# Gathering an expert layer's rows in two halves of slots instead of two halves of row groups, on one Trainium2 core

## The chip, the cores and the metric

The kernel runs on one core of a Trainium2 chip. The metric is the device time of one execution in microseconds (us); of the kernel before, three runs are shown. Engines are called by their names: TensorE (PE in the profile, its weight loads PEld), VectorE (DVE), ScalarE (ACT), GpSimd (POOL) and SyncE (SP, whose queue issues the DMAs).

## The reference

A two-layer encoder trunk over 256 tokens of width 1024. Each layer has a mixer (retention and chunked attention, or sliding-window attention), a hierarchical mixture of experts, and a gated per-layer embedding. The change lies in the mixture of experts:

```python
def hierarchical_moe(h, w_group, b_group, w_router, b_router, w_gate, w_up, w_down):
    t = h.reshape(b * s, d)
    g_logits = t @ w_group + b_group
    g_onehot = one_hot(argmax(g_logits))                    # 1 of 4 groups
    e_logits = einsum('td,dge->tge', t, w_router) + b_router
    top_v, top_i = top_k(einsum('tge,tg->te', e_logits, g_onehot), 2)   # 2 of its 4 experts
    gates = ...                                             # softmax weights, per token and expert
    for gi in range(4):
        hg = einsum('td,edf->tef', t, w_gate[gi])           # 1024 -> 512
        hu = einsum('td,edf->tef', t, w_up[gi])
        act = silu(hg) * hu * gates[:, gi, :, None]
        out = out + einsum('tef,efd->td', act, w_down[gi])  # 512 -> 1024
```

Every token goes to 2 of 16 experts, so there are 512 (token, expert) slots per layer.

## The kernel before, in words

Each engine has a program of its own, written out by hand in the order of its work, and the programs meet at semaphores. The order is fixed on every engine: what stands behind a wait waits too.

**The expert stage.** The router gives every slot a place, sorted by expert. The normalised rows of the tokens (1024 features = 8 row groups of 128, features k, k+8, k+16, ... in group k) are brought into slot order by TensorE: one-hot matrices `PH` (tile `gather_onehots`, tokens x 512 slots, two token tiles `t`) are the moving operand, and the token rows `HSP` (tile `rows_split`, a high and a low part, read in steps of `KD` = 8 elements) the stationary one. A row group takes four matmuls (two token tiles, two parts), of 512 columns each, into a bank of its own. ScalarE and VectorE copy the sums, multiplied by the norm's weights, to `XS` (tile `normalised`). From there ScalarE copies each expert's block of 64 slots to `XE` (tile `expert_rows`), and TensorE runs gate and up (`gate_up`: for each of 8 groups two matmuls, 16 records per half of the groups), turns the hidden rows (`turned`), runs down (`down`) and scatters the outputs back to tokens (`scatter`). All of these but gather and scatter are fp32 matmuls, which the profile shows as two records each.

**The order around the change** (in `experts` of TensorE's program): after the side product (line 926) the gather of groups 0 to 3, token tile 0 (`gathered_first(0)`), the opening of the second tile's sums (`open_sums(1)`, line 935), groups 0 to 3, token tile 1; then the first halves (groups 0 to 3) of gate and up of experts 0 and 1 (`first_rows`), the gather of groups 4 to 7 (`gathered`), the second half of expert 0 (`other_rows(0)`), `spread` (slots and gates broadcast to all partitions), the second half of expert 1. Then the experts follow one another in `step`. Expert 0's block of groups 0 to 3 has copies of its own (`first_block`, 64 columns), since whole evacuations take longer. The one-hots are made by VectorE, 512 wide, token tile 0 and then 1 (lines 1972 and 1973), in front of the low parts of row groups 4 to 7 (`rows_low(1, 4, KD)`, line 1875).

**The weights.** 16 experts x 3 matrices of 2 MiB per layer pass through nine slots of `weights` in SBUF. SP issues their transfers in a fixed order, and each waits until the matrix before it in its slot has been used; experts 0 to 5, 14 and 15 and all down matrices move in pieces of 1 MiB, which wait for half matrices. Two signals count here: `gate_up_halves` (an expert's first four groups are done) and `gate_up_ready` (all eight). For experts 3 and 4 the order is

```python
for half in range(2):
    load_part(3, 1, half)   # reuses expert 0's gate
    load_part(4, 0, half)   # reuses expert 0's up
    load_part(4, 1, half)   # reuses expert 1's gate
    load_part(3, 2, half)   # reuses expert 1's up
```

Ahead of it SP stores the side product (three transfers, `side_first_stored` to `side_third_stored`; it lies where `XS` will be written) and loads expert 2's down matrix outside the slots (`outside` to tile `residual`, the rest to `weights_rest`).

## Time and profile before

| | us |
|---|---|
| median of three runs | 727.9 (726.28 to 727.92) |
| the profiled execution, own time | 727.73 |
| its span, first to last instruction | 725.9 |
| TensorE busy | 706.7 (97%) |
| VectorE busy | 301.5 (42%) |
| ScalarE busy | 166.1 (23%) |
| bytes moved by DMA | 250.87 MB, mean 346 GB/s |

The expert stages take the time from about 147 to 356 us and from about 480 to 689 us of the span. A row of the windows view gives busy time and count for each engine, then the granted TensorE clock (1.00 is 2.4 GHz, 0.50 is 1.2 GHz), the mean busy share of the 16 DMA engines and what they moved. Ends of matmul records are modelled, so starts are the better guide.

### The profile page before, as it was taken

How to read it: one execution, taken by the hardware profiler on the slowest of the kernel's cores; microseconds unless marked ns; L12 is line 12 of the kernel's file. 1: busy time of each engine (PE TensorE's matmuls, PEld its weight loads, DVE VectorE, ACT ScalarE, POOL GpSimd, SP SyncE). 2: the span in 40 equal slices, each digit the busy share in tenths (PEclk: the TensorE clock that was granted, in tenths of full speed). 3: DMA queues.
4: the chain of work that ended last, by engine and by line, in shares of the span. 5: the costliest groups of instructions: out<-in, count | busy, mean ns of one | idle time of the engine just before them, and what ended most of it. 6: DMA issues, size and time to landing. Idle time of an engine off the chain costs nothing.

```text
span 725.9 us, 8170 instructions
## 1 busy us (share of the span) xinstructions
PE 706.7 (97%) x3062; PEld 328.4 (45%) x3062; DVE 301.5 (42%) x717; ACT 166.1 (23%) x395; POOL 26.4 (4%) x47
## 2 busy tenths in 40 slices
PE   9999999999999999989999999999999999989996
PEld 5488454564333333333445545455333333333344
DVE  1213361545437343433322557263535534324324
ACT  3000241432111111110331144252111111112132
POOL 0500000000000000000000000000000000000000
PEclk9999999999999999999999999999999999999999
DMA  9998448889999999999999851489999999999941
GB/s 344 376 285 293 184 174 328 331 310 367 421 409 424 424 431 424 426 418 422 398 381 409 328 197 79 180 284 355 412 412 426 429 422 424 428 420 422 406 164 59
DMA packets 46056, 250.87 MB, mean 346 GB/s; under 512 B 4200, under 2 KB 5448, under 8 KB 25536
## 3 DMA queue, kind: packets, MB, share of 16 engines
q1 hardware_dynamic: 43648, 245.04, 84.4%
q0 software_dynamic: 2048, 5.07, 2.2%
q8 instruction: 26, 0.43, 0.2%
q10 hardware_dynamic: 320, 0.22, 0.1%
q14 instruction: 14, 0.11, 0.0%
HBM read 247.15 MB, written 4.73 MB: 347 GB/s over the span
## 4 chain that ended last, share of the span: by engine, by line
PE 81%; DMA 9%; SPq 5%; issue 2%; DVE 2%; ACT 1%; POOLq 0%; POOL 0%; ACTq 0%; DVEq 0%
PE bank L1024 25%; PE bank L699 24%; PE bank L1041 12%; SPq L454 4%; DMA weights<-in_moe_w_up_dram 4%; PE bank L732 4%; DMA weights<-in_moe_w_down_dram 4%; PE bank L1049 3%; PE bank L983 2%; PE bank L926 2%; PE bank L684 1%; PE bank L1033 1%; DMA weights<-in_even_w_in_dram 1%; PE bank L712 1%; PE bank L770 0%
## 5 line engine op out<-in xcount | busy, mean ns | idle before, releaser
L1024 PE MATMUL bank<-weights,expert_rows 128*64 128x512 f32 x992 | 222.5, 600 | 6.2 <-DMA weights<-in_moe_w_up_dram 6.2
L699 PE MATMUL bank<-weights,normalised 128*128 128x512 f32 (+1 forms) x448 | 191.4, 580 | 0.9 <-DVE normalised L1699 0.7
L1024 PEld LDWEIGHTS bank<-weights,expert_rows 128*64 128x64 f32 x992 | 73.7, 138 | 147.1 <-issue 145.8
L699 PEld LDWEIGHTS bank<-weights,normalised 128*128 128x128 f32 x448 | 83.1, 190 | 91.4 <-issue 88.5
L1041 PE MATMUL bank<-weights,hidden_turned_odd 128*64 128x512 f32 x256 | 58.8, 598 | 0.4 <-DMA weights<-in_moe_w_down_dram 0.4
L1041 PE MATMUL bank<-weights,hidden_turned 128*64 128x512 f32 x224 | 51.5, 598 | 1.3 <-DVE hidden_turned L2029 0.6
L1534 ACT ACTIVATE gate_tanh<-bank 128x256 f32<-128x256 f32 x32 | 12.3, 384 | 175.2 <-PE bank L1024 175.2
L1385 ACT ACTIVATE expert_outputs<-bank 64x512 fp32r<-64x512 f32 (+1 forms) x32 | 18.9, 591 | 117.7 <-PE bank L1041 112.3
L2029 DVE COPY hidden_turned<-bank 128x256 f32<-128x256 f32 x16 | 6.8, 424 | 75.0 <-PE bank L1033 75.0
L2060 DVE TENSOR_TENSOR expert_outputs<-bank,expert_outputs 64x512 fp32r<-64x512 f32 x30 | 20.5, 684 | 41.7 <-ACT expert_outputs L1385 41.5
L2029 DVE COPY hidden_turned_odd<-bank 128x256 f32<-128x256 f32 x16 | 6.8, 424 | 63.3 <-PE bank L1033 63.1
L1041 PEld LDWEIGHTS bank<-weights,hidden_turned_odd 128*64 128x64 f32 x256 | 16.9, 136 | 34.8 <-issue 31.7
L2041 DVE SCALAR_TENSOR_TENSOR spread_gates<-token_slots,router_temps,token_gates 128x512 f32<-128x512 f32 x32 | 24.0, 751 | 12.9 <-ACT token_gates L1526 11.9
L1041 PEld LDWEIGHTS bank<-weights,hidden_turned 128*64 128x64 f32 x224 | 15.2, 136 | 29.2 <-issue 28.9
L732 PE MATMUL bank<-normalised,weights 128*128 128x256 f32 x128 | 28.4, 380 | 0.0
L1049 PE MATMUL bank<-expert_outputs,scatter_onehots 128*128 128x512 f32 x60 | 26.1, 436 | 0.2
L732 PEld LDWEIGHTS bank<-normalised,weights 128*128 128x128 f32 x128 | 24.1, 190 | 3.7 <-issue 0.5
L1049 PE MATMUL bank<-gather_onehots,scatter_onehots 128*128 128x512 f32 x60 | 23.6, 394 | 0.0
L2044 DVE TENSOR_REDUCE slot_gates<-spread_gates 128x1 f32<-128x512 f32 x32 | 21.9, 686 | 1.1
L1385 ACT ACTIVATE expert_rows<-normalised 128x512 f32 (+1 forms) x32 | 19.5, 611 | 10.9 <-issue 6.9
L1033 PEld LDWEIGHTS bank<-constants,hidden 128*128 128x128 f32 x64 | 10.1, 206 | 26.3 <-issue 24.7
L1381 ACT ACTIVATE normalised<-bank,norm_weights 128x128 f32<-128x128 f32 x48 | 13.7, 368 | 33.3 <-PE bank L684 33.0
(276 smaller groups left out, 647.1 us busy)
## 6 DMA issues: line engine op xcount, KB each, us to landing
weights<-in_moe_w_down_dram SPq DMA_DIRECT2D x60, 1024.0 KB, 19.6
weights<-in_moe_w_gate_dram SPq DMA_DIRECT2D x32, 1024.0 KB, 8.7
weights<-in_moe_w_up_dram SPq DMA_DIRECT2D x32, 1024.0 KB, 10.1
weights<-in_moe_w_gate_dram SPq DMA_DIRECT2D x16, 2048.0 KB, 16.5
weights<-in_moe_w_up_dram SPq DMA_DIRECT2D x16, 2048.0 KB, 21.0
weights<-in_even_w_in_dram SPq DMA_DIRECT2D x5, 2048.0 KB, 20.4
weights<-in_ple_w_gate_dram SPq DMA_DIRECT2D x4, 2048.0 KB, 31.5
weights<-in_even_w_out_dram SPq DMA_DIRECT2D x2, 2048.0 KB, 32.5
```

The costliest lines, as they stand in the source:

```text
L454: sp.dma_start(dst, src).then_inc(done, 16)
L699: mm = pe.matmul(B[bank][:, 0:width], XT[:, k, tok(t)], w[:, k, :], start=(k == 0), stop=(k == KD - 1))
L732: mm = pe.matmul(B[2 * (u % 2) + pair][:, c * SEQ:(c + 1) * SEQ], w[:, k, tok(2 * pair + c)], XT[:, k, :], start=(k == 0), stop=(k == KD - 1))
L926: mm = pe.matmul(B[4 + 2 * t + half][:, :], PINT[:, k, tok(t)], WPL[k][:, half * 512:(half + 1) * 512], start=(k == 0), stop=(k == 1))
L1024: mm = pe.matmul(bank[j * BLK:(j + 1) * BLK, :].rearrange("p (m f) -> p m f", m=2), rows[:, k, :], W[:, slots, a:a + FF // 2], start=(k == ...
L1033: mm = pe.transpose(B[TURNED_BANK][:, c * P:(c + 1) * P], US[:, c:2 * P:2], ident)
L1041: mm = pe.matmul(bank[half * BLK:(half + 1) * BLK, :], hid[:, 2 * (f % 2) + f // 2, :], rows(f)[:, half * 512:(half + 1) * 512], start=(f ...
L1049: return pe.matmul(B[sum_bank(t, half)][:, :], PT2[:, par, tok(t)], YSPLIT[half][:, par, :], start=False, stop=stop)
L1385: return act.activation(dst, src, ACT.Copy)
L2041: stepped(dve.scalar_tensor_tensor(out=SPREAD, in0=SROW.rearrange("p c s -> p (c s)"), scalar=col, in1=WROW.rearrange("p c s -> p (c s)"), ...
L2044: stepped(dve.tensor_reduce(GATES[:, par:par + 1], SPREAD, AX.X, ALU.add), gates)
L2060: return dve.tensor_tensor(YSPLIT[half][low, par, :], bank[high, :], YSPLIT[half][high, par, :].bitcast(F32), ALU.subtract)
```

## The change

The gather is divided the other way: by slots instead of by row groups. First slots 0 to 255 of all eight groups, in pairs of groups that share a bank; then the whole gate and up of expert 0 (its 64 slots are in place in `XS`, and nothing is copied for it); then slots 256 to 511 of all eight groups; then expert 1's first half, the spread, and its second half. Each matmul has 256 columns, and there are twice as many, since each half uses the stationary operands anew. The one-hots are made in the same halves. Evacuations are 256 wide (16 instead of 8, without the four 64-wide copies per layer). SP issues the transfer to `weights_rest` behind the last side store. `rows_bank`, `in_bank`, `by_act` and `evac_count` say which bank, half of a bank, engine and count belong to a group.

```diff
-def rows_bank(k):
-    return (0, 1, 4, 5, 1, 4, 1, 4)[k]
+def rows_bank(half, k):
+    return ((0, 1, 4, 5), (5, 4, 1, 4))[half][k // 2]
+def in_bank(k):
+    return slice(256 * (k % 2), 256 * (k % 2) + 256)
+def by_act(k):
+    return k in (0, 1, 4, 5)
+def evac_count(half, k):
+    return 4 * half + 2 * (k // 4) + k % 2 + 1
...
 # SP
-                        sp.wait_ge(sem("side_ready"), 4 * l + 4)
+                        sp.wait_ge(sem("side_copied"), 4 * l + 4)
+                        side_half_stored(1)
                         sp.dma_start(XD[:, :], srcs[2][l * NE + 2][0:256, :].rearrange("(p c) d -> p (c d)", c=2))\
                             .then_inc(sem("down2_landed"), 16)
-                        sp.wait_ge(sem("side_copied"), 4 * l + 4)
-                        side_half_stored(1)
...
 # TensorE
-                def gathered_part(k, t):
-                    for part in range(2):
-                        mm = pe.matmul(B[rows_bank(k)][:, :], HSP[part][:, t, k:D:KD], PH[:, t, :], start=(t + part == 0),
-                                       stop=(t + part == TT))
+                def gathered(half, k):
+                    for t in range(TT):
+                        for part in range(2):
+                            mm = pe.matmul(B[rows_bank(half, k)][:, in_bank(k)], HSP[part][:, t, k:D:KD],
+                                           PH[:, t, 256 * half:256 * half + 256], start=(t + part == 0), stop=(t + part == TT))
+                    mm.then_inc(sem("rows_ready"), 1)
+                def gathered_first():
+                    pe.wait_ge(sem("onehots_ready"), 4 * l + 2)
+                    pe.wait_ge(sem("hs_low"), 3 * l + 2)
+                    pe.wait_ge(sem("side_copied"), 4 * l + 2)
+                    for k in range(4):
+                        gathered(0, k)
+                    pe.wait_ge(sem("side_copied"), 4 * l + 4)
+                    open_sums(1)
+                    pe.wait_ge(sem("hs_low"), 3 * l + 3)
+                    for k in range(4, KD):
+                        gathered(0, k)
+                def gathered_second():
+                    pe.wait_ge(sem("onehots_ready"), 4 * l + 4)
+                    for k in range(KD):
+                        if k == 0:
+                            pe.wait_ge(sem("rows_by_dve"), 8 * l + evac_count(0, 7))
+                        elif k == 2:
+                            pe.wait_ge(sem("rows_by_act"), 8 * l + evac_count(0, 5))
+                        elif k == 6:
+                            pe.wait_ge(sem("rows_by_dve"), 8 * l + evac_count(1, 3))
+                        gathered(1, k)
...
+                def first_expert():
+                    wait_unit(u0)
+                    wait_unit(u0 + 1)
+                    gate_up(B[gu_bank(0)], XS[:, :, 0:BLK], pair(u0), lambda: wait_second(u0, u0 + 1), sem("gate_up_halves"),
+                            row_ready=row_in_place).then_inc(sem("gate_up_ready"), 1)
...
-                gathered_first(0)
-                pe.wait_ge(sem("side_copied"), 4 * l + 4)
-                open_sums(1)
-                gathered_first(1)
-                first_rows(0)
-                first_rows(1)
-                for k in range(4, KD):
-                    for t in range(TT):
-                        gathered(k, t)
-                other_rows(0)
+                gathered_first()
+                first_expert()
+                gathered_second()
+                second_expert(0)
                 spread()
-                other_rows(1)
+                second_expert(1)
...
 # ScalarE
+                def rows_evac(half, k):
+                    act.wait_ge(sem("rows_ready"), 16 * l + 8 * half + k + 2 - k % 2)
+                    act.activation(XS[:, k, 256 * half:256 * half + 256], B[rows_bank(half, k)][:, in_bank(k)], ACT.Copy,
+                                   scale=NW[:, kn, k:k + 1]).then_inc(sem("rows_by_act"), 1)
+                act.wait_ge(sem("side_first_stored"), 16 * (l + 1))
+                rows_evac(0, 0)
+                rows_evac(0, 1)
+                for half in range(2):
+                    seed(1, half)
+                act.wait_ge(sem("onehots_ready"), 4 * l + 4)
+                rows_evac(0, 4)
+                rows_evac(0, 5)
...
 # VectorE
-                for t in range(TT):
-                    then(dve.tensor_scalar(TMP[:, t, :], IOTA, S2[:, t, :], None, ALU.is_equal))
-                    dve.scalar_tensor_tensor(out=PH[:, t, :], in0=IOTA, scalar=S1[:, t, :], in1=TMP[:, t, :],
-                                             op0=ALU.is_equal, op1=ALU.add).then_inc(sem("onehots_ready"), 1)
+                def gather_onehots(half):
+                    c = slice(256 * half, 256 * half + 256)
+                    for t in range(TT):
+                        then(dve.tensor_scalar(TMP[:, t, c], IOTA[:, c], S2[:, t, :], None, ALU.is_equal))
+                        dve.scalar_tensor_tensor(out=PH[:, t, c], in0=IOTA[:, c], scalar=S1[:, t, :], in1=TMP[:, t, c],
+                                                 op0=ALU.is_equal, op1=ALU.add).then_inc(sem("onehots_ready"), 1)
+                gather_onehots(0)
+                rows_low(1, 4, KD)
+                gather_onehots(1)
...
+                rows_evac(0, 2)
+                dve.wait_ge(sem("side_second_stored"), 16 * (l + 1))
+                rows_evac(0, 3)
+                rows_evac(0, 6)
+                dve.wait_ge(sem("side_third_stored"), 16 * (l + 1))
+                rows_evac(0, 7)
```

The order on TensorE in layer 0, from the last side matmul (`ple_weights_first`, `weights_rest` are its weights) to expert 1's second half. A row is a line, an operation, its tiles (`normalised` there is `XS`), the output's shape and the count of matmuls. Before:

```order
L926 MATMUL bank<-weights_rest,arena 128x512
L983 MATMUL bank<-gather_onehots,rows_split 128x512 x8
L935 MATMUL bank<-zero_column 128x512 x2
L983 MATMUL bank<-gather_onehots,rows_split 128x512 x8
L1024 MATMUL bank<-weights,expert_rows 64x512 x16
L983 MATMUL bank<-gather_onehots,rows_split 128x512 x16
L1024 MATMUL bank<-weights,normalised 64x512 x8
L1010 MATMUL bank<-constants,router_temps 128x128 x4
L1012 MATMUL bank<-constants,router_temps 128x128 x4
L1024 MATMUL bank<-weights,expert_rows 64x512 x8
```

And now:

```order
L940 MATMUL bank<-weights_rest,arena 128x512
L998 MATMUL bank<-gather_onehots,rows_split 128x256 x16
L949 MATMUL bank<-zero_column 128x512 x2
L998 MATMUL bank<-gather_onehots,rows_split 128x256 x16
L1047 MATMUL bank<-weights,normalised 64x512 x16
L998 MATMUL bank<-gather_onehots,rows_split 128x256 x32
L1047 MATMUL bank<-weights,expert_rows 64x512 x8
L1033 MATMUL bank<-constants,router_temps 128x128 x4
L1035 MATMUL bank<-constants,router_temps 128x128 x4
L1047 MATMUL bank<-weights,expert_rows 64x512 x8
```

Expert 1's first half, which was beside expert 0's, now stands behind all of the gather; expert 0's second half stands ahead of the gather's last 32 matmuls.

SP's queue in layer 0 from the first side store to experts 3 and 4's pieces, each row with what it waits for. Before:

```order
L503 DMA side_product_dram<-normalised 128x1024 [waits side_copied]
L478 DMA residual<-in_moe_w_down_dram 128x1024 [waits hs_low,seeded]
L482 DMA side_product_dram<-normalised 128x512 [waits side_copied]
L510 DMA weights_rest<-in_moe_w_down_dram 128x2048 [waits side_ready]
L482 DMA side_product_dram<-normalised 128x512 [waits side_copied]
L478 DMA residual<-in_moe_w_down_dram 128x1024 [waits hs_low,seeded]
```

And now, with the eight pieces behind it, whose order is as before:

```order
L518 DMA side_product_dram<-normalised 128x1024 [waits side_copied]
L493 DMA residual<-in_moe_w_down_dram 128x1024 [waits hs_low,seeded]
L497 DMA side_product_dram<-normalised 128x512 [waits side_copied] x2
L526 DMA weights_rest<-in_moe_w_down_dram 128x2048
L493 DMA residual<-in_moe_w_down_dram 128x1024 [waits hs_low,seeded]
L469 DMA weights<-in_moe_w_up_dram 128x2048 [waits gate_up_halves]
L469 DMA weights<-in_moe_w_gate_dram 128x2048 [waits gate_up_halves]
L469 DMA weights<-in_moe_w_up_dram 128x2048 [waits gate_up_halves]
L469 DMA weights<-in_moe_w_down_dram 128x2048 [waits gate_up_halves]
L469 DMA weights<-in_moe_w_up_dram 128x2048 [waits gate_up_ready]
L469 DMA weights<-in_moe_w_gate_dram 128x2048 [waits gate_up_ready]
```

Only the transfer to `weights_rest` has moved here; the first two pieces wait for expert 0's first half, the next two for expert 1's, the last two shown for expert 0's second.

## Rows read from the trace of the kernel before

**Rows 1.** The page, busy us (share of the span) and instructions of each engine.
```profile
PE 706.7 (97%) x3062; PEld 328.4 (45%) x3062; DVE 301.5 (42%) x717; ACT 166.1 (23%) x395; POOL 26.4 (4%) x47
```

**Rows 2.** Chain of waits, 130 to 180 us: start us, us, what.
```profile
147.31 1.95 PE bank L983 x8
...
149.66 2.27 PE bank L983 x8
151.94 7.02 PE bank L1024 x32
158.96 4.62 PE bank L983 x16
163.57 3.58 PE bank L1024 x16
...
168.25 0.91 PE bank L1012 x8
```

**Rows 3.** Windows: length, busy us (count) per engine, PE clock, DMA share, GB/s.
```profile
155.00:157.00 2.00, 2.00 (x12) 0.65 (x10) 1.15 (x8) 0.00 (x0) 0.00 (x0) 1.00 0.32 61
157.00:167.00 10.00, 10.00 (x42) 5.63 (x38) 1.50 (x2) 1.80 (x3) 0.00 (x0) 1.00 0.98 402
167.00:169.00 2.00, 2.00 (x18) 1.86 (x16) 0.00 (x0) 0.00 (x0) 0.00 (x0) 1.00 0.56 127
169.00:176.00 7.00, 6.20 (x30) 2.29 (x30) 5.46 (x11) 2.90 (x6) 0.00 (x0) 1.00 0.97 366
...
180.00:350.00 170.00, 166.72 (x754) 60.73 (x752) 71.98 (x152) 29.09 (x54) 0.00 (x0) 0.99 1.01 421
```

**Rows 4.** TensorE's waits for weights: timeline of layer 0, a window, layer 1's waits.
```profile
311.34 8.71 PE L1024 MATMUL bank<-weights,expert_rows 128*64 128x512 f32 x32 [2.72 <-DMA weights<-in_moe_w_up_dram]
...
351.34 1.94 PE L1041 MATMUL bank<-weights,hidden_turned_odd 128*64 128x512 f32 x8 [0.42 <-DMA weights<-in_moe_w_down_dram]
...
311.30:314.80 3.50, 3.46 (x10) 1.20 (x12) 0.00 (x0) 0.00 (x0) 0.00 (x0) 0.52 1.03 426
...
PE bank L1024 <- DMA weights<-in_moe_w_up_dram: 3.0, 2, 2.7
```

**Rows 5.** Loads of gather and scatter (ns min/median/max), then timeline from 149.5 us.
```profile
L983 PEld LDWEIGHTS bank<-gather_onehots,rows_split x64: 312/330/348, 146.7 to 496.6; 128*128 128x128 f32 x64
...
L1049 PEld LDWEIGHTS bank<-gather_onehots,scatter_onehots x60: 187/188/192, 184.8 to 686.9; 128*128 128x128 f32 x60
...
149.59 2.35 PE L983 MATMUL bank<-gather_onehots,rows_split 128*128 128x512 f32 x8
...
149.81 1.81 PEld L983 LDWEIGHTS bank<-gather_onehots,rows_split 128*128 128x128 f32 x7
```

**Rows 6.** Timeline of TensorE, two scatter matmuls that follow one another.
```profile
185.03 0.39 PE L1049 MATMUL bank<-gather_onehots,scatter_onehots 128*128 128x512 f32 x1
185.26 0.40 PE L1049 MATMUL bank<-expert_outputs,scatter_onehots 128*128 128x512 f32 x1
```

**Rows 7.** Timeline of VectorE: one-hots, low parts, evacuation, 256-wide one-hots.
```profile
145.37 0.49 DVE L1972 TENSOR_SCALAR normalised<-normalised,router_temps 128x512 f32<-128x512 f32 x1
...
148.12 0.73 DVE L1875 SCALAR_TENSOR_TENSOR rows_split<-residual,norm_stats,rows_split 128x512 fp32r<-128x512 f32 x1
...
161.33 0.75 DVE L1991 TENSOR_SCALAR normalised<-bank,norm_weights 128x512 f32<-128x512 f32 x1 [5.01 <-PE bank L983]
...
172.65 0.35 DVE L2048 TENSOR_SCALAR spread_gates<-token_slots,router_temps 128x256 f32<-128x256 f32 x1
173.04 0.48 DVE L2049 SCALAR_TENSOR_TENSOR scatter_onehots<-token_slots,router_temps,spread_gates 128x256 fp32r<-128x256 f32 x1
```

**Rows 8.** Timeline of SP's queue: first, second and last pair of issues.
```profile
155.56 0.33 SPq L454 DMA_DIRECT2D weights<-in_moe_w_up_dram  x1
...
159.00 0.33 SPq L454 DMA_DIRECT2D weights<-in_moe_w_up_dram  x1
...
172.76 0.33 SPq L454 DMA_DIRECT2D weights<-in_moe_w_up_dram  x1
```

More of the change, by code:

```diff
@@ L1159, in other_rows @@
-                def other_rows(e):
-                    n = u0 + 3 * e
-                    if e == 1:
-                        pe.wait_ge(sem("xe_ready"), NE * l + 2)
-                    gate_up(B[gu_bank(e)], XS[:, :, 0:BLK] if e == 0 else XE[:, e], pair(n), lambda: wait_second(n, n + 1), None, (1,),
-                            first_block if e == 0 else None).then_inc(sem("gate_up_ready"), 1)
-                gathered_first(0)
-                pe.wait_ge(sem("side_copied"), 4 * l + 4)
-                open_sums(1)
@@ new lines, in second_expert @@
+                def second_expert(half):
+                    n = u0 + 3
+                    if half == 0:
+                        pe.wait_ge(sem("xe_first"), l + 1)
+                        pe.wait_ge(sem("rows_by_act"), 8 * l + evac_count(1, 1))
+                        wait_unit(n)
+                        wait_unit(n + 1)
+                        gate_up(B[gu_bank(1)], XE[:, 1], pair(n), None, sem("gate_up_halves"), (0,))
+                    else:
+                        pe.wait_ge(sem("xe_ready"), NE * l + 2)
+                        gate_up(B[gu_bank(1)], XE[:, 1], pair(n), lambda: wait_second(n, n + 1), None, (1,))\
+                            .then_inc(sem("gate_up_ready"), 1)
@@ L1482, in experts @@
                             seed(0, half)
-                for half in range(2):
-                    seed(1, half)
                 def rows(e, off=None, part=slice(0, KD), done="xe_ready", count=1):
@@ new lines, in experts @@
+                act.wait_ge(sem("side_first_stored"), 16 * (l + 1))
[6 more added lines that the diff above has]
+                rows_evac(0, 5)
+                act.wait_ge(sem("g_below_max"), l + 1)
+                act.activation(RT[:, 20:28], RT[:, 20:28], ACT.Exp).then_inc(sem("g_exp"), 1)
+                act.wait_ge(sem("second_below_first"), l + 1)
@@ L1503, in experts @@
+                act.activation(RT[:, 84:86], RT[:, 84:86], ACT.Exp).then_inc(sem("second_exp"), 1)
                 act.wait_ge(sem("table_ready"), 2 * l + 1)
                 offs = act.value_load(TBL[0:1, 1:2], min_val=0, max_val=LAST)
-                if l == 1:
-                    act.wait_ge(sem("gate_up_ready"), NE * l - 1)
-                for half in range(2):
-                    for k in (4 * half, 4 * half + 2):
-                        if half == 0:
-                            first_block(k)
-                        else:
-                            act.wait_ge(sem("rows_ready"), 8 * l + k + 1)
-                        if k == 0:
-                            act.wait_ge(sem("side_first_stored"), 16 * (l + 1))
-                        rows_evac(k)
-                    act.wait_ge(sem("rows_by_act"), 4 * l + 2 * half + 2)
-                    act.wait_ge(sem("rows_by_dve"), 4 * l + 2 * half + 2)
-                    rows(1, offs, slice(4 * half, 4 * half + 4), ("xe_first", "xe_ready")[half], (1, 2)[half])
-                    if half == 0:
-                        act.wait_ge(sem("g_below_max"), l + 1)
-                        act.activation(RT[:, 20:28], RT[:, 20:28], ACT.Exp).then_inc(sem("g_exp"), 1)
-                        act.wait_ge(sem("second_below_first"), l + 1)
-                        act.activation(RT[:, 84:86], RT[:, 84:86], ACT.Exp).then_inc(sem("second_exp"), 1)
@@ L1524, in experts @@
+                for part in range(2):
+                    rows_evac(1, 4 * part)
+                    rows_evac(1, 4 * part + 1)
+                    act.wait_ge(sem("rows_by_act"), 8 * l + evac_count(1, 4 * part + 1))
+                    act.wait_ge(sem("rows_by_dve"), 8 * l + evac_count(1, 4 * part + 3))
+                    rows(1, offs, slice(4 * part, 4 * part + 4), ("xe_first", "xe_ready")[part], (1, 2)[part])
                 act.wait_ge(sem("srow_ready"), l + 1)
@@ L2067, in low_parts @@
                         low_part(bank, e % 2, half).then_inc(sem("ys_low_ready"), 1)
[L2069 to L2073 removed]
+                for k in (2, 3, 6, 7):
+                    rows_evac(1, k)
                 dve.wait_ge(sem("srow_copied"), l + 1)
```

61 lines of the change are left out of this document (8 added, 53 removed).

## The prediction

> **What bounds the kernel now.** I read the page first, then the chain of waits of layer 0's expert stage, the windows of the same stretch, TensorE's idle rows, and last the single lines. The page says that TensorE is busy 97% of the span [rows 1], so time added to TensorE is time unless it was waiting anyway. The chain from 147 to 169 us [rows 2] is TensorE alone: the gather in three pieces (1.95, 2.27 and 4.62 us = 8.84 us for 32 matmuls), the first halves of experts 0 and 1 (7.02 us, so 3.51 each), expert 0's second half (3.58, to 167.15), the spread (to 168.25 + 0.91 = 169.16, so 2.0 us) and then expert 1's second half. Nothing else ends a step there.
>
> The windows show the second bound [rows 3]. Between 180 and 350 us the DMA engines are full (share 1.01) at 421 GB/s, so a piece of 1 MiB (half of a weight matrix) takes 2.49 us, and nothing lost before that stretch can be made up inside it. Between 155 and 176 us they are not full. Held against 421 GB/s, the four windows lack 2 x (1 - 61/421) = 1.7 us, 10 x (1 - 402/421) = 0.45, 2 x (1 - 127/421) = 1.4 and 7 x (1 - 366/421) = 0.9: 4.5 us of transfer time lost. That the transfers decide the end is seen in TensorE's waits [rows 4]: 2.72 us for expert 13's weights at 311 us, and 0.42 us at 351.34 us for the second half of the last down matrix, the last unit of the layer. So the end of layer 0's expert stage is set by DMA, with no slack at the last unit. After the 2.72 us of idling the granted clock is 0.52, the 1.2 GHz level, for 3.5 us, and that matrix takes 8.71 us, where an undisturbed one takes about 7.1. Layer 1 is the same: 3.0 us of such waits for gate and up weights.
>
> **TensorE's part.** The change replaces 32 gather matmuls of 512 columns by 64 of 256. The stationary operand (128 tokens of one row group, read in steps of eight elements) is the same one in both halves, and each half loads it again: 32 loads become 64. What does such a pair cost? In the steady stretch seven loads begin within 1.81 us including the last one's 0.33, so one every (1.81 - 0.33)/6 = 0.247 us [rows 5]. Is that the moving operand or the load? The scatter moves the same 512 columns of the same type, but its stationary operand is contiguous: its load takes 188 ns where the gather's takes 330 [rows 5], and its matmuls follow one another 0.23 us apart [rows 6]. The gather is slower than the scatter by its load, so the load sets its pace, and halving the columns takes nothing from it. I take 0.246 us for each of the 64. The ends: 0.22 us, if a 256-column matmul disturbs the load less (where no gather matmul runs yet, two loads start 149.81 - 149.59 = 0.22 apart, the first with the group of matmuls [rows 5]); below, half of the scatter's 0.23 with some gap, 0.125, if the load were hidden altogether.
>
> The Trainium skill (TensorE: Matmul & The Clock Gate, section LDWEIGHTS) makes a load cost its columns at 1.2 GHz, 107 ns for 128, whatever its stride, and lets it be pulled ahead of running matmuls; by it a pair would be bound by the 256 moving columns, the gather would cost nothing more, and this is the rival "hidden loads" below. The same skill (SBUF — State Buffer, section Door 1: The DMA port swizzle, its note on cachelines) says that each step to a new 16-byte line pays a penalty; a step of eight fp32 elements is 32 bytes, which is the side that the trace takes.
>
> Now the path. The first gather matmul can start at 147.31 as before: the one-hots are now made 256 wide, and rows of that width take 0.35 and 0.48 us and start 0.39 apart [rows 7], so the four of the first half end at 145.37 + 0.39 + 0.40 + 0.39 + 0.48 = 147.0. The low parts of row groups 4 to 7 (0.73 us [rows 7]) come next, ready at 147.8, wanted near 151.7; the second half's one-hots end near 149.5, wanted at 163. They cost nothing; if VectorE were 0.5 us late there, TensorE would lose just that.
> - Gather, slots 0 to 255: 32 x 0.246 = 7.87, plus 0.41 for opening the sums (the step between the first two gather rows [rows 2]), plus 0.2 for a load that has nothing to hide behind: ends at 155.8.
> - Expert 0 whole, 2 x 3.51: first half done at 159.3 (before 155.5), all at 162.8 (before 167.2). An evacuation of 256 columns can't take longer than the 0.75 us of a whole row group [rows 7]; even so groups 6 and 7, the last, are in place by 157.5, and wanted from 161 on.
> - Gather, slots 256 to 511: 7.87 + 0.2, ends at 170.9. Before, the last 16 matmuls took 4.62 instead of 16 x 0.247 = 3.95 because they waited for banks; the new order of banks takes these waits away, and that is in the sum.
> - Expert 1's first half 3.51 (174.4), spread 2.0 (176.4), second half 3.51: 179.9. Before: 169.15 + 3.51 = 172.66.
>
> TensorE is thus 7.25 us later per layer. The removed 64-wide copies of expert 0 and halved evacuations are ACT's and VectorE's; TensorE did not wait for them, so I cost them at nothing, and the router arithmetic behind them (ends near 159 instead of 155) is wanted only by the spread at 174.
>
> **The DMA queue's part.** SP issues in a fixed order: after experts 3 and 4's pieces that reuse expert 0's first halves come two that reuse expert 1's first halves, and only then those that reuse expert 0's second halves. Before, these were issued at 155.56, 159.00, 167.20 and 172.76 us, two pieces each [rows 8, 3], and data flows some 1.5 us after the issue (61 GB/s until 157). Now: the first two at 159.4, flowing from 160.9 to 165.9; the next not before expert 1's first half is done, 174.5, flowing from 176.0. That expert 0's second halves are free at 162.8, 4 us sooner than before, helps nobody, as they stand behind that wait. From 176 on six pieces keep the engines busy 15 us, and the rest follows in time. Lost: 155.2 to 160.9 and 165.9 to 176.0 = 5.7 + 10.1 = 15.8 us, against 4.5 before. The transfers are **11.3 us** late per layer, 4 us more than TensorE, and since the last unit has no slack, the stage ends 11.3 us later. The 4 us show up as longer waits for weights in experts 11 to 15. The weights_rest transfer, issued behind the side store 0.6 us later, and the last piece of residual, issued 2 us later because ScalarE now opens sums behind the gather, only shift idle time before 155; they are wanted only in expert 2's down step, after experts 0 to 3 have passed.
>
> Sum: 2 x 11.3 = 22.6 us on the profiled execution's 727.73 us, 0.2 below the median shown: **750 us**. With 0.22 us per pair each layer saves 64 x 0.026 = 1.7: 747.
>
> **The rivals.**
> - Hidden loads: a pair takes 0.125. For it speaks that loads run beside matmuls; against it the 330 against 188 ns. TensorE would be 8.0 + 0.4 = 8.4 instead of 8.84 us (and 0.2 from gaps: 0.7 earlier at expert 1's end). The queue would still lose: first issue at 155.3, next at 166.5, idle 155.2 to 156.8 and 161.8 to 168.0 = 7.8 against 4.5, so +3.3 per layer: 734.3.
> - TensorE's lateness fills its own waits: if the transfers were not put off, 7.25 us late would swallow the 3.6 us of waits and the 1.6 us of slow clock, +2.1 per layer: 731.8. Against it: the issue order above.
> - Not slower: pairs below 0.13 us (where 64 x p + 0.4 falls under 8.84) and a queue that stays no tighter than before, so that only TensorE's 0.7 us per layer are left: 726.3. It decides only if both hold; the 4.5 us that the queue lacks now would have to be TensorE's doing alone.
> - New stalls: two groups now share a bank and leave it together. If evacuations hold the gather up as before (0.7 us a layer), and one more stretch at 1.2 GHz (1.6 us a layer) falls behind the last long DMA wait, 750 becomes 755.
>
> **How the numbers follow.** The forecast gets 0.76 (own range 746 to 754), new stalls 0.07, hidden loads 0.09, filled waits 0.04, not slower 0.04. The range 734 to 756 takes in the first three. A difference of 0.3% (2.2 us) is about what a measurement of this kernel tells from none. Only the fourth rival lies below: 0.02 faster, 0.02 same, 0.96 slower.
>
> **What would show it.** Gather loads still near 330 ns and 0.245 apart, 16, 16 and 32 of them in 3.9, 3.9 and 7.9 us. Expert 0's gate and up in one stretch beginning near 155.8. SP issuing at about 159.4 and then nothing until 174.5; two holes in the DMA windows, near 156 to 161 and 166 to 176. TensorE 7 us late at expert 1's end and 11 us late at the end of each expert stage, with DMA waits of 8 us or so instead of 3.6. A pace near 0.13 would make it wrong in the first term, a stage that ends 7 us late or less in the second.

## The result and the profile after

The changed kernel takes **748.08 us** (median of 4 runs, 747.75 to 748.68), the kernel before in the same comparison 727.91 us (4 runs, 726.28 to 729.18). The ratio is 1.0279 with a 95% interval of 1.0258 to 1.0301: 2.8% slower, +20.2 us. The profiled execution took 748.10 us with a span of 746.3 us (before: 727.73 and 725.9), so the two traces differ by 20.4 us. A trace is of one execution; the times are medians of several.

The page of the changed kernel: engines, and the group of the gather's loads (busy us, mean ns, then the idle time before them).

```profile
PE 722.4 (97%) x3126; PEld 346.3 (46%) x3126; DVE 303.2 (41%) x729; ACT 167.1 (22%) x399; POOL 26.4 (4%) x47
...
L998 PEld LDWEIGHTS bank<-gather_onehots,rows_split 128*128 128x128 f32 x128 | 31.3, 337 | 3.3 <-issue 2.1
```

TensorE is busy 15.7 us longer than in [rows 1] and its share is 97% as before: by shares alone nothing changed. The loads are 128 where there were 64, at 337 ns each.

The chain of waits of the changed kernel in layer 0, from the first gather matmul to the spread (start us, us, what), and the first piece of layer 1's gather:

```profile
148.05 3.91 PE bank L998 x16
151.96 0.41 PE bank L949 x2
152.37 4.04 PE bank L998 x16
156.41 7.02 PE bank L1047 x32
163.43 7.90 PE bank L998 x32
171.33 3.58 PE bank L1047 x16
...
176.00 0.91 PE bank L1035 x8
...
491.29 3.90 PE bank L998 x16
```

Held against [rows 2], whose pieces are 1.95, 2.27 and 4.62 us, the gather takes 3.91 + 4.04 + 7.90 = 15.85 us where it took 8.84. No wait for banks stands between the pieces. The one-hots are only just in time:

```profile
147.28 0.48 DVE L1984 SCALAR_TENSOR_TENSOR gather_onehots<-normalised,router_temps 128x256 fp32r<-128x256 f32 x1
```

The last one of the first half is done at 147.76, and the timeline has the first gather record at 147.82; experiment 1, whose one-hots are made as before, takes 3.73 us for the same 16 matmuls, so at most 0.2 us is lost here. Expert 1's second half begins at 176.91 (before: 169.16), and its row of the timeline ends at 180.48 (before: 172.72). Counted from each kernel's own first gather matmul that is 32.43 us, before 172.72 - 147.31 = 25.41: **7.0 us** more.

Windows of the changed kernel (length, busy us per engine, clock, DMA share, GB/s):

```profile
156.00:161.00 5.00, 5.00 (x24) 1.85 (x25) 3.76 (x21) 0.41 (x2) 0.00 (x0) 1.00 0.14 49
161.00:166.00 5.00, 5.00 (x23) 3.22 (x20) 0.00 (x0) 0.40 (x2) 0.00 (x0) 1.00 0.99 362
166.00:176.00 10.00, 10.00 (x49) 7.35 (x49) 1.75 (x4) 2.11 (x6) 0.00 (x0) 1.00 0.10 35
176.00:360.00 184.00, 177.95 (x805) 66.30 (x805) 81.09 (x168) 32.95 (x61) 0.00 (x0) 0.99 1.01 422
```

SP's queue in the same stretch of the changed kernel (each row one issue):

```profile
160.04 0.33 SPq L469 DMA_DIRECT2D weights<-in_moe_w_up_dram  x1
...
174.96 0.33 SPq L469 DMA_DIRECT2D weights<-in_moe_w_up_dram  x1
175.33 0.43 SPq L469 DMA_DIRECT2D weights<-in_moe_w_down_dram  x1
175.81 0.43 SPq L469 DMA_DIRECT2D weights<-in_moe_w_up_dram  x1
```

Two pieces go out at 160 us and then nothing until 174.96, where [rows 8] has issues at 155.56, 159.00, 167.20 and 172.76. The windows show the two holes that follow: 49 GB/s for 5 us and 35 GB/s for 10 us, and full engines (422 GB/s) behind them for 184 us. Expert 0's second halves had been free since 163.43; the piece that goes into one of them is the row of 175.81, 12 us later, behind the two that wait for expert 1's first half.

The rest of the stage on TensorE (timeline of the changed kernel, idle time before the row in brackets):

```profile
292.48 7.09 PE L1047 MATMUL bank<-weights,expert_rows 128*64 128x512 f32 x32 [0.40 <-DMA weights<-in_moe_w_up_dram]
...
307.24 8.79 PE L1047 MATMUL bank<-weights,expert_rows 128*64 128x512 f32 x32 [2.72 <-DMA weights<-in_moe_w_up_dram]
...
322.00 7.09 PE L1047 MATMUL bank<-weights,expert_rows 128*64 128x512 f32 x32 [1.03 <-DMA weights<-in_moe_w_up_dram]
...
346.84 3.65 PE L1047 MATMUL bank<-weights,expert_rows 128*64 128x512 f32 x16 [0.99 <-DMA weights<-in_moe_w_up_dram]
...
361.66 1.94 PE L1064 MATMUL bank<-weights,hidden_turned_odd 128*64 128x512 f32 x8 [0.46 <-DMA weights<-in_moe_w_down_dram]
...
366.49 1.16 PE L698 MATMUL bank<-constants,residual 128*128 128x128 f32 x8 [0.39 <-DVE residual L1718]
```

The five waits for weights sum to 5.6 us; before there were three, 3.6 us: 2.72 and 0.42 [rows 4] and one of 0.45 at 296.59. The stage ends at the last row shown, 218.44 us after the first gather matmul, where before it was 356.18 - 147.31 = 208.87: **+9.57 us**. In layer 1 it is 709.65 - 491.29 = 218.36 against 689.28 - 480.96 = 208.32: **+10.04**. The other 0.75 us of the 20.4 is a shift: the first gather matmul starts at 148.05 and not at 147.31, and the last side matmuls ahead of it are late by as much. It comes from the first 15 us of the span, where both kernels run the same program. The same row of TensorE's timeline, before and now:

```profile
14.41 6.17 PE L699 MATMUL bank<-weights,normalised 128*128 128x512 f32 x14
```

```profile
15.16 5.31 PE L713 MATMUL bank<-weights,normalised 128*128 128x512 f32 x12
```

From that row to the last side matmuls both traces take 131.87 us. Between the layers the two kernels are equal, 123.78 and 123.76 us from the end of layer 0's stage to layer 1's last side matmuls.

### The profile page after: what moved, and what is told of

Read it like the earlier page. It is cut to its first block, busy times and chain, and to the rows that moved or that the text cites. A ratio compares the mean times of both kernels' runs of the same rounds, so it can differ in the third digit from the quotient of the medians.

```text
span 746.3 us, 8308 instructions
## 1 busy us (share of the span) xinstructions
PE 722.4 (97%) x3126; PEld 346.3 (46%) x3126; DVE 303.2 (41%) x729; ACT 167.1 (22%) x399; POOL 26.4 (4%) x47
## 4 chain that ended last, share of the span: by engine, by line
PE 70%; DMA 15%; SPq 10%; issue 2%; DVE 2%; ACT 1%; POOLq 0%; POOL 0%; ACTq 0%; DVEq 0%
PE bank L713 24%; PE bank L1047 18%; SPq L469 10%; DMA weights<-in_moe_w_up_dram 8%; PE bank L1064 7%; DMA weights<-in_moe_w_down_dram 7%; PE bank L998 4%; PE bank L746 4%; PE bank L940 2%; PE bank L1072 2%; PE bank L698 2%; PE bank L726 1%; PE bank L1056 1%; PE bank L852 1%; PE bank L784 0%
## 5 line engine op out<-in xcount | busy, mean ns | idle before, releaser
L1047 PE MATMUL bank<-weights,expert_rows 128*64 128x512 f32 x960 | 215.9, 601 | 10.9 <-DMA weights<-in_moe_w_up_dram 10.9
L998 PEld LDWEIGHTS bank<-gather_onehots,rows_split 128*128 128x128 f32 x128 | 31.3, 337 | 3.3 <-issue 2.1
L998 PE MATMUL bank<-gather_onehots,rows_split 128*128 128x256 f32 x128 | 32.5, 409 | 0.0
L1399 ACT ACTIVATE expert_rows<-normalised 128x512 f32 (+1 forms) x32 | 19.6, 611 | 15.3 <-issue 10.9
## 6 DMA issues: line engine op xcount, KB each, us to landing
weights<-in_moe_w_gate_dram SPq DMA_DIRECT2D x16, 2048.0 KB, 19.6
```

Source lines behind the costliest of these rows:

```text
L998: mm = pe.matmul(B[rows_bank(half, k)][:, in_bank(k)], HSP[part][:, t, k:D:KD], PH[:, t, 256 * half:256 * half + 256], start=(t + part == ...
L1047: mm = pe.matmul(bank[j * BLK:(j + 1) * BLK, :].rearrange("p (m f) -> p m f", m=2), rows[:, k, :], W[:, slots, a:a + FF // 2], start=(k == ...
L1399: return act.activation(dst, src, ACT.Copy)
```

## The experiments

The change does three things at once: it doubles the gather's loads, it leaves SP's order of issues as it was while the order of TensorE's work is another, and it moves one-hots, copies and banks. The experiments undo or do one at a time. Two marks are read in each: the first down matmul (TensorE's lateness at the head of the stage) and the transposes behind the stage (its end), both counted from the start of the last pair of side matmuls ahead of the gather, layer 0 / layer 1. The changed kernel is +7.0 / +7.0 us at the first and +9.6 / +10.0 at the second. Ratios are to the kernel before in the same comparison, with their 95% interval.

**1. Only the loads.** The kernel before, with each 512-column gather matmul as two of 256 that load the same operand; order, banks, copies and queue untouched.

```diff
-    mm = pe.matmul(B[rows_bank(k)][:, :], HSP[part][:, t, k:D:KD], PH[:, t, :], start=(t + part == 0),
-                   stop=(t + part == TT))
+    for n in range(2):
+        c = slice(256 * n, 256 * n + 256)
+        mm = pe.matmul(B[rows_bank(k)][:, c], HSP[part][:, t, k:D:KD], PH[:, t, c], start=(t + part + n == 0),
+                       stop=(t + part + n == TT + 1))
```

> The kernel before, its order untouched, but each gather matmul of 512 columns is two of 256 (64 per layer), so each stationary operand is loaded twice. Theory (the strided load of 0.25 us sets the pace): loads start 0.246 apart, the gather takes about 16 us instead of 8.8, TensorE is 7.2 us late at expert 1's end; the queue's order fits this order of work, so its transfers are as late as TensorE and no more, and the time rises by about 2 x 7 = 14 us to 742. Rival (loads are hidden, the change's loss is all order): no load costs more, 728. Rival (TensorE's lateness fills its own DMA waits): 2 x 2 = 4 us, 732.

Measured: 741.57 us, ratio 1.0199 [1.0184, 1.0215]. First down +6.9 / +6.9, stage end +6.6 / +6.6. Its chain of waits:

```profile
147.62 3.73 PE bank L985 x16
...
151.77 4.06 PE bank L985 x16
155.83 7.02 PE bank L1026 x32
162.85 7.93 PE bank L985 x32
```

Its loads in the view by lines (ns min/median/max):

```profile
L985 PEld LDWEIGHTS bank<-gather_onehots,rows_split x128: 312/337/341, 147.0 to 510.4; 128*128 128x128 f32 x128
```

The pieces are nearly those of the changed kernel. Doubling the loads alone costs 13.9 us of the 20.2, 6.6 per layer, with no change in where the work stands, as expected; both rivals (728 and 732) are out. Here the stage's end is late by no more than TensorE's head. SP's queue says why:

```profile
162.89 0.33 SPq L454 DMA_DIRECT2D weights<-in_moe_w_up_dram  x1
...
174.40 0.33 SPq L454 DMA_DIRECT2D weights<-in_moe_w_up_dram  x1
```

The second pair of pieces goes out at 162.89, as soon as expert 1's first half is read (155.83 + 7.02), and not at 174.96.

**2. Only the queue's order undone.** The changed kernel, with SP's loop split so that the pieces reusing expert 0's halves are issued before any that reuse expert 1's.

```diff
 for half in range(2):
     load_part(3, 1, half)
     load_part(4, 0, half)
+for half in range(2):
     load_part(4, 1, half)
     load_part(3, 2, half)
```

> The changed kernel, but SP issues the pieces that reuse expert 0's second halves ahead of those that reuse expert 1's first halves. TensorE's program is as changed. Theory (the queue's fixed order makes the transfers 4 us later than TensorE): the issues for expert 0's second halves come at about 163.5 instead of 175.8, the hole from 166 to 176 shrinks by 5 us, TensorE is still 7.1 us late at expert 1's end, its later waits fall back to those of before, and the time falls by 6 to 8.5 us to 740 to 742. Rival (TensorE's lateness alone makes the loss, the holes don't matter): 748, no change.

Measured: 741.13 us, 1.0187 [1.0171, 1.0202]; first down +7.0 / +7.0, stage end +7.2 / +6.6. SP's queue of this kernel:

```profile
162.27 0.33 SPq L469 DMA_DIRECT2D weights<-in_moe_w_up_dram  x1
...
173.75 0.33 SPq L469 DMA_DIRECT2D weights<-in_moe_w_up_dram  x1
```

The issues stand where experiment 1 has them, TensorE is as late as in the changed kernel, and 7.0 us are gone (748.08 - 741.13). Of these, 2.4 and 3.4 lie in the two stages, and 1.2 ahead of layer 0's gather, which begins at 146.85 here and at 148.05 in the changed kernel. That part is not the edit's: the row of the changed kernel at 15.16 stands at 13.95 in this trace, and all eleven traces, whose program is the same up to there, lie between the two. By the stages the change's 19.6 us divide into 13.2 for the loads (experiment 1, both layers) and 5.9 for two DMA pieces queued behind a wait that had nothing to do with them (this one). About half a microsecond of the stages is left open. The window from 150 to 176 us puts the same into bytes. Before, experiment 1, experiment 2, and the changed kernel, in this order:

```profile
150.00:176.00 26.00, 25.20 (x116) 13.18 (x117) 11.74 (x36) 7.84 (x18) 0.00 (x0) 1.00 0.88 334
```

```profile
150.00:176.00 26.00, 26.00 (x119) 18.05 (x119) 6.27 (x25) 5.42 (x12) 0.00 (x0) 1.00 0.64 239
```

```profile
150.00:176.00 26.00, 26.00 (x120) 17.75 (x121) 6.39 (x27) 5.15 (x13) 0.00 (x0) 1.00 0.64 233
```

```profile
150.00:176.00 26.00, 26.00 (x117) 18.06 (x117) 6.73 (x32) 5.72 (x14) 0.00 (x0) 1.00 0.47 159
```

At 422 GB/s (the changed kernel's full rate) its 159 against 334 is 26 x 175/422 = 10.8 us of transfer time; experiment 1 lacks 5.9 and experiment 2 lacks 6.2.

**3. The stationary operand laid out contiguously.** The changed kernel, with the split rows stored as (row group, 128 columns) instead of every eighth element. The work of spreading them goes to the engines that write them.

```diff
-HSP = [HL[:, part] for part in range(2)]
+HSP = [HL[:, part].rearrange("p t (k m) -> p t k m", k=KD) for part in range(2)]
...
-    mm = pe.matmul(B[rows_bank(half, k)][:, in_bank(k)], HSP[part][:, t, k:D:KD],
+    mm = pe.matmul(B[rows_bank(half, k)][:, in_bank(k)], HSP[part][:, t, k, :],
...
-act.activation(HSP[0][:, t, :], H[:, t, :], ACT.Copy, scale=rstd(kn, t))
+act.activation(HSP[0][:, t], H[:, t, :].rearrange("p (m k) -> p k m", k=KD), ACT.Copy, scale=rstd(kn, t))
```

> The changed kernel, but the tokens' high and low rows are written group by group, so that a stationary operand of the gather is 128 contiguous elements; nothing else is moved. Theory (the stride makes the load slow): loads fall from 337 to about 190 ns, the matmuls start 0.12 to 0.13 apart, the gather takes 8.2 us instead of 16, TensorE reaches expert 1's end 0.7 us before the kernel before; the queue's order still makes the transfers about 3 us late per layer: 733 to 735. Rival (the number of loads or a floor for 256 columns sets the pace, whatever the stride): 748. Rival (the strided reads of ScalarE and VectorE that now write these rows are slow): loads are fast, but the gather starts later than the side matmuls' end.

Measured: 738.03 us, 1.0141 [1.0126, 1.0157]. First down -0.4 / -0.4, stage end +2.4 / +2.7. Loads and ScalarE's copies by lines (ns min/median/max):

```profile
L998 PEld LDWEIGHTS bank<-gather_onehots,rows_split x128: 186/192/192, 148.2 to 504.3; 128*128 128x128 f32 x128
...
L1482 ACT ACTIVATE rows_split<-residual,norm_stats x4: 2147/2166/2173, 129.9 to 480.5; 128x1024 fp32r<-128x1024 f32 x4
```

The chain of waits at layer 0's gather, and TensorE's timeline ahead of layer 1's stage:

```profile
148.47 1.94 PE bank L998 x16
...
159.95 2.13 PE bank L998 x16
...
162.18 0.89 DVE normalised L1999 x2
```

```profile
473.47 0.40 PE L927 MATMUL bank<-constants,router_temps 128*128 128x20 f32 x2 [1.98 <-DVE router_temps L1889]
473.71 3.66 PE L713 MATMUL bank<-weights,normalised 128*128 128x512 f32 x4
```

The window over those four matmuls has a granted clock of 0.54:

```profile
473.70:477.40 3.70, 3.70 (x7) 1.64 (x7) 1.42 (x6) 0.00 (x0) 0.00 (x0) 0.54 0.02 4
```

The load took 192 ns where it took 337, and 16 gather matmuls 1.94 us instead of 3.91, with everything else of the change in place. That is the direct proof that the stride of the load sets the pace; 7.2 and 7.3 us per layer go with it, and the 2.4 and 2.7 that stay go with the queue's order (experiment 4). With the loads fast the banks begin to matter: ahead of its last 8 matmuls the gather waits 1.0 us, to 163.11, for VectorE's copies out of a bank (`normalised`, the row at 162.18), so the first down matmul is only 0.4 us early. The expected 733 to 735 was missed by 3 us or more, and its second rival, that the engines which now write these rows are slow, came true: ScalarE's copies take 2.17 us where they took 1.16, VectorE's of 512 elements 1.2 where it was 0.75, and they stand ahead of TensorE. Layer 1's stage begins 4.3 us later (TensorE waits 1.98 us for router arithmetic that is queued behind a copy, and the next four matmuls then run at half the clock, 3.66 us against 1.98), layer 0's 0.7 us later: from ScalarE's first copy to the last side matmuls it is 17.57 us, in the traces that leave the copies contiguous 16.83. The strided access was not removed but moved to two other engines, which are slow at it too.

**4. Both.** Experiment 3 with experiment 2's loop.

> The changed kernel with contiguous stationary operands and the other queue order together. Theory: both terms are gone; TensorE 0.7 us earlier at expert 1's end than before the change and the transfers no later, so 726.5, 1 to 2 us under the kernel before. If only one of the two causes were real, the time would be that of the better of the two single runs.

Measured: 731.07 us, 1.0042 [1.0028, 1.0056]. First down -0.4 / -0.4, stage end -0.7 / -0.7: with the loads fast and the queue in order, the stage itself is shorter than before in both layers, and nothing of the +9.6 and +10.0 is left to explain. Against experiment 3 the queue's order alone is worth 3.1 and 3.4 us. The expected 726.5 was missed by the same 0.7 and 4.2 us ahead of the two gathers.

**5. Runs of four elements.** The changed kernel with rows in two blocks of four groups, so that ScalarE and VectorE move runs of four and the load's step is 4 elements instead of 8.

```diff
+HSP = [HL[:, part].rearrange("p t (q m r) -> p t q m r", q=2, r=4) for part in range(2)]
...
+    mm = pe.matmul(B[rows_bank(half, k)][:, in_bank(k)], HSP[part][:, t, k // 4, :, k % 4],
```

> The changed kernel with the token rows kept in two blocks of four row groups, so that a stationary operand is read in steps of four elements (16 bytes) and ScalarE and VectorE read and write runs of four. In e3_contiguous ScalarE's and VectorE's steps of eight elements cost 1 us each time, 1 us of delay ahead of layer 0's gather and 4.3 us ahead of layer 1's. Theory (one step per 16-byte line is still free): loads near 190 ns, ScalarE's rows near 1.2 us, VectorE's near 0.75 per 512, gather matmuls 0.13 apart, and with the queue's order as changed the stages 2.1 to 2.4 us longer than in the kernel before (as in e3): 732 to 733. Rival (only steps that hit a line twice are free): loads stay at 330 ns and the time near 748.

Measured: 747.51 us, 1.0277 [1.0262, 1.0293], the changed kernel again. Its loads and copies:

```profile
L998 PEld LDWEIGHTS bank<-gather_onehots,rows_split x128: 308/332/334, 147.0 to 513.2; 128*128 128x128 f32 x128
...
L1482 ACT ACTIVATE rows_split<-residual,norm_stats x4: 1149/1162/1162, 129.4 to 483.4; 128x1024 fp32r<-128x1024 f32 x4
```

The expected 732 to 733 was missed, and the rival (748) held: the load is as slow with a step of four (332 ns) as with eight, while ScalarE pays nothing for runs of four (1.16 us).

**6. The same layout in the kernel before.**

> The kernel before with the same layout of the token rows and nothing else. Theory: its gather matmuls start 0.231 instead of 0.246 apart, 32 x 0.015 = 0.5 us less per layer in the gather, and the transfers follow: 727, not to be told from before. Rival (steps of four are slow): 728 with loads at 330 ns. If the layout costs ScalarE or VectorE time, the gather starts later and the time rises over 728.

Measured: 727.56 us (11 runs) against 727.28, 1.0006 [0.9997, 1.0015]: no difference. The loads take 310 ns, as the rival had it (before: 330), and not 190.

**7. Steps of four, the queue's order, and banks in another turn** ((4, 5, 1, 4) instead of (5, 4, 1, 4) for the second half, with its waits).

> The changed kernel with three edits: rows in steps of four, expert 0's second halves issued first, and the second half's banks in the order 4, 5, 1, 4 (in e3 the faster gather waited 1.0 us for VectorE's evacuation of bank 4; now it waits for ScalarE's, two groups earlier). Theory: stages 1.1 us (as in e4) to 2 us shorter than before and the gather starting on time: 724 to 726. Rival (steps of four are slow): 741, as e2_queue_order.

Measured: 741.43 us, 1.0195 [1.0181, 1.0209], as experiment 2; the expected 724 to 726 was missed because the loads stayed slow (330 ns), and the rival (741) held. The other turn of the banks gains nothing while the loads are slow.

**8. Steps of two, the queue's order, those banks.** Rows in four blocks of two groups: the load steps by two elements, VectorE's low parts are cut into instructions of 256 elements.

```diff
+HSP = [HL[:, part].rearrange("p t (q m r) -> p t q m r", q=4, r=2) for part in range(2)]
...
+    mm = pe.matmul(B[rows_bank(half, k)][:, in_bank(k)], HSP[part][:, t, k // 2, :, k % 2],
```

> As e7_all, but the token rows lie in four blocks of two row groups: a stationary operand is read in steps of two elements, ScalarE and VectorE read and write runs of two, and VectorE's low parts are 256 elements per instruction. Theory (a load is fast as long as each 16-byte line is hit twice): loads near 200 ns, the gather 8.2 us, and, if runs of two are free for ScalarE and VectorE, 724 to 727. Rival (any step slows the load): 741, as e7_all. Rival (runs of two are slow for ScalarE): as e4_both, 729 to 731.

Measured: 727.80 us (11 runs) against 727.41 (21 runs), 1.0004 [0.9995, 1.0013]; expected were 724 to 727. Loads and copies by lines:

```profile
L999 PEld LDWEIGHTS bank<-gather_onehots,rows_split x128: 193/196/199, 146.7 to 495.1; 128*128 128x128 f32 x128
...
L1483 ACT ACTIVATE rows_split<-residual,norm_stats x4: 1230/1240/1246, 129.1 to 472.4; 128x1024 fp32r<-128x1024 f32 x4
```

The chain of waits at the gather:

```profile
146.98 1.96 PE bank L999 x16
...
158.49 4.04 PE bank L999 x32
```

An operand with a step of two loads in 196 ns and costs ScalarE 7% (1.24 us). The last 32 gather matmuls take 4.04 us without a wait for a bank. All 20 us are back: first down -0.7 / -0.7, stage end -1.2 / -0.9. Of these 2.1 us, 0.5 is lost between the layers (TensorE waits 0.7 us for router arithmetic where it waited 0.2, here and in experiment 9). The traced execution keeps the rest: it took 725.91 us, 1.8 less than the traced one before. But it is the fastest of its 11, whose median is 0.4 us above that of the kernel before. So the gain is one of a single execution and not shown for the kernel.

**9. Steps of two in the kernel before.**

> The kernel before with the rows in four blocks of two groups and nothing else. Theory: loads near 200 ns, matmuls of 512 columns 0.231 apart, 0.5 us less per layer, 726 to 727; it says whether the changed order gains anything once the loads are cheap: e8_step2_all below e9_step2_before if it does.

Measured: 726.87 us (11 runs), 0.9996 [0.9987, 1.0005]: no difference. TensorE reaches the first down 0.65 us sooner in both layers; the stage ends 1.3 us sooner in layer 0 and 1.1 later in layer 1. Its loads take 194 ns. The waits for gate and up weights in the whole run (total us, times, longest) say where the gain goes, here and in the kernel before:

```profile
PE bank L1024 <- DMA weights<-in_moe_w_up_dram: 7.7, 4, 2.7
```

```profile
PE bank L1024 <- DMA weights<-in_moe_w_up_dram: 6.2, 4, 2.7
```

TensorE is sooner and waits 1.5 us more for them; the 0.4 us for the last down matrix [rows 4] is gone. No version measured is faster than the kernel before by more than the interval, and with cheap loads the new order (experiment 8, 727.80) is no better than the old one (9, 726.87).

## Why the prediction was right

748.08 lies 1.9 us under the forecast of 750.0 and inside its own range. The mechanism held in both terms. The number is a little closer than the terms are: the two stages are 19.6 us longer, not 22.6, and the 0.75 us of shift, which is no part of the change, makes up some of the difference. By the steps:

- **The loads set the pace: held.** 0.246 us per pair was predicted. In the changed kernel 18 loads begin within 4.44 us, (4.44 - 0.34)/17 = 0.241, and with 16 pairs in 3.91 us, 0.244. Experiment 1 shows that the pairs alone do it, experiment 3 that the stride does: 337 ns fell to 192 and the gather to 1.94 us for 16. The rival "hidden loads" is excluded by the first. Its price was right for another layout: with a load of 192 ns a pair takes 0.12 to 0.13 us (1.94 and 2.13 for 16).
- **The rule on loads.** The Trainium skill (TensorE: Matmul & The Clock Gate, section LDWEIGHTS) prices a load by its columns alone, with no term for a stride, 107 ns for 128. The trace disagrees twice: a contiguous operand takes 192 ns, and a step costs more, 196 ns with two, 332 with four, 337 with eight. Of the Trainium skill's note on 16-byte lines (SBUF — State Buffer, section Door 1: The DMA port swizzle) the trace bears out one half and not the other. Full speed needs two hits in each line, it says, and that fits: a step of two fp32 elements has them and costs next to nothing, a step of four has one and is as slow as eight. That four fp32 elements can be stepped for free, as it says too, is not so for this load.
- **TensorE's path: held.** Forecast +7.25 us at expert 1's end, measured +7.0. The one-hots of the first half are done at 147.76, 0.06 us ahead of the first gather record, and cost at most 0.2 us. Evacuated rows were in place at 157.3, as assumed (157.5). The waits for banks did go, as 32 matmuls in 7.90 us show.
- **The queue: held in its issues.** Forecast 159.4 and 174.5 from a gather at 147.31; measured 160.04 and 174.96, which less the shift of 0.74 is 159.3 and 174.2. Two holes, as forecast. Experiment 2 shows what the order of issues has in them: of the 10.8 us of transfer time lost, 6.2 stay with the order undone, as long as the loads keep TensorE late, and some 4.6 go with it.
- **The step that was mis-sized** is "the transfers are 11.3 us late per layer ... and since the last unit has no slack, the stage ends 11.3 us later". The stage ends 9.6 and 10.0 us later. Half a microsecond is the hole itself, 10.8 us by the windows and not 11.3. Counted by bytes from the records of the transfers and with the shift taken off, lateness stays there: 10.8 us at 250 us, 10.7 at 350. But the last unit lets TensorE go at 361.66 against 351.34, only 9.6 us later without the shift. The term took the last unit to land at the same count of bytes in both kernels, and it does not: when it landed, 125.89 MB had moved before and 125.45 MB in the changed kernel, so fewer bytes of later transfers were ahead of it, 0.44 MB or 1.0 us at 422 GB/s. In the traces of experiments 1 to 9 the count lies between 125.56 and 125.96 MB, so this microsecond may be one of single executions rather than of the change. Whether the same holds in layer 1 is open.
- **The waits** came out at 5.6 us in layer 0 and 5.7 in layer 1, not "8 us or so". The forecast added the 4 us between TensorE's lateness and the stage's to the 3.6 us of before; these 4 us were 2.5 and 3.0, and the waits rose by 2.0 and 2.7 (before: 3.6 and 3.0).
- **The other rivals.** "Filled waits" had the transfers not put off: the kernel in which that holds is nearest experiment 2, and even there the stage was 6.6 to 7.2 us late, the same as TensorE, because with slow loads the issues are late as well. "New stalls" did not come: no bank stall, and one stretch at half the clock in each layer, as before. "Not slower" needs both cheap pairs and a queue no tighter; experiment 8 supplies both, and is 1.0004 of the time before (experiment 4 does too, and pays ahead of the gathers). That both are needed was right: experiments 2 and 3 supply one each and are 1.9% and 1.4% slower.

The 0.75 us of shift ahead of layer 0's gather was in no term, and rightly: it is there by 15 us of the span, where the eleven traces, all of the same program up to there, scatter by 1.2 us. What sets it in those first 15 us is open; marks within a layer are the safer comparison.

The move of the weights_rest transfer behind the side store was predicted to cost nothing and not tried by itself. Experiment 2 contains it and 1 does not; they are 0.4 us apart, which is no proof, since they differ in the order of work as well.

## What to carry to other kernels

When a matmul is cut along its moving columns, count its weight loads and look at how long one of them takes and how far apart they start: if the load sets the pace already, halving the columns nearly doubles the time (8.84 us became 15.85), and here the layout of the stationary operand decided more than the tiling. When work is reordered on one engine, reorder every in-order queue that waits for its results; here a transfer whose buffer was free waited 12 us behind one whose buffer was not. And where a strided read is made contiguous, look at who writes it: the price can return on an engine ahead.

## What the chip showed that I had not expected

- The step at which a load becomes slow lies between two and four fp32 elements, and there is hardly a further price from four to eight: 192, 196, 332 and 337 ns for steps of one, two, four and eight.
- ScalarE and VectorE see the same layouts differently. For 1024 elements ScalarE takes 1.16 us with runs of four, 1.24 with runs of two and 2.17 with single elements eight apart; VectorE takes 0.75 us for 512 with runs of four, 0.95 with runs of two (two instructions of 0.48) and 1.2 with single ones. So a layout exists (runs of two) that is cheap for TensorE and ScalarE, and whose price on VectorE did not reach the time here.
- A wait of 2.72 us was followed in the changed kernel's layer 0 by a stretch at the 1.2 GHz level (granted 0.55 over 307.2 to 310.7 us; 32 matmuls in 8.79 us instead of 7.09), and waits of 0.40, 1.03 and 0.99 us were not. In layer 1 two waits of the same length went both ways, and in experiment 3 one of 1.98 us was enough. Only the rows with their granted clock tell; the length of the wait does not. The two waits of layer 1, then the windows behind them (the clock is the third number from the end):

```profile
650.32 7.09 PE L1047 MATMUL bank<-weights,expert_rows 128*64 128x512 f32 x32 [2.73 <-DMA weights<-in_moe_w_up_dram]
...
665.07 8.78 PE L1047 MATMUL bank<-weights,expert_rows 128*64 128x512 f32 x32 [2.72 <-DMA weights<-in_moe_w_up_dram]
```

```profile
650.30:653.80 3.50, 3.48 (x17) 1.45 (x19) 0.00 (x0) 0.00 (x0) 0.00 (x0) 1.00 1.03 428
665.00:668.50 3.50, 3.43 (x10) 1.29 (x12) 0.00 (x0) 0.00 (x0) 0.00 (x0) 0.63 1.00 417
```
